# Hybrid encoder layer on one core: output projection by seven block products, second norm in two token halves, first weight sums spread through the recurrent heads

## What is computed

```python
mod = silu(c) @ w_ada + b_ada                      # shift, scale, gate, twice
h = rms_norm(x, norm_mix_pre) * (1 + sc1) + sh1
aq, ak, av, hq, hf_f, hf_b, hi, hg = split(h @ w_in)
o_att = attention_group(aq, ak, av, q_norm, k_norm)         # 8 heads, 1024 columns
o_hg = hgrn2_group(hq, hf_f, hf_b, hi, hg, ...)             # 8 recurrent heads, 1024 columns
mix = concatenate([o_att, o_hg]) @ w_out           # 512 tokens x 2048 by 2048 x 2048
x = x + g1 * rms_norm(mix, norm_mix_post)
h = rms_norm(x, norm_ffn_pre) * (1 + sc2) + sh2    # the second norm
x = x + g2 * rms_norm(conv_glu_ffn(h), norm_ffn_post)
```

## Time and profile before

| | |
|---|---|
| median of 3 runs | 2378.76 us (2375.49 to 2380.01) |
| span of the profiled execution | 2375.8 us |
| TensorE busy | 98% |
| VectorE busy | 79% |
| ScalarE busy | 47% |
| last head's loop and output projection | 840.4 to 1034.1 us |
| seam and first up rows | 1034.1 to 1075.2 us |

### The profile page before, as it was taken

One profiled execution on the slowest core, in us unless ns is written; L12 is line 12 of the kernel. 1 busy time (PEld: TensorE's weight loads), 2 busy tenths in 40 slices (PEclk: granted clock), 3 DMA queues, 4 the chain that ended last, 5 costly groups with the idle time before them and its releaser, 6 DMA issues.

```text
span 2375.8 us, 37218 instructions
## 1 busy us (share of the span) xinstructions
PE 2334.7 (98%) x13671; PEld 2025.8 (85%) x13671; DVE 1878.8 (79%) x2447; ACT 1104.8 (47%) x1517; POOL 128.6 (5%) x207
## 2 busy tenths in 40 slices
PE   6999999999999999999999999999999999999998
PEld 3577778888888877878999999999999998888887
DVE  5875667887777873267799999999999998888777
ACT  4266744334443353254444444444444445555554
POOL 1010000000000000000000000000000000001100
PEclk9999999999999999999999999999999999999999
DMA  9952456666666734336555555555555559779966
GB/s 366 346 157 85 133 180 208 215 219 212 207 211 198 234 89 169 98 124 159 146 140 146 145 144 143 144 142 139 141 145 145 142 176 329 251 207 285 279 226 224
DMA packets 378834, 442.47 MB, mean 186 GB/s; under 512 B 14876, under 2 KB 295716, under 8 KB 376448
## 3 DMA queue, kind: packets, MB, share of 16 engines
...
...
## 4 chain that ended last, share of the span: by engine, by line
PE 87%; DVE 5%; DMA 3%; ACT 2%; issue 2%; SPq 0%; DVEq 0%; ACTq 0%
PE bank L2132 26%; PE bank L2134 26%; PE bank L2133 26%; DMA ADA<-in_w_ada_dram 2%; PE bank L2295 2%; DVE ACC L1373 2%; DMA AB_raw<-in_w_ada_dram 1%; PE bank L2198 1%; DVE ZZ L1577 1%; PE bank L2375 1%; PE bank L2314 1%; PE bank L2189 1%; DVE W_lo L1332 0%; PE bank L2063 0%; DVE AB_acc L1636 0%
## 5 line engine op out<-in xcount | busy, mean ns | idle before, releaser
L2132 PE MATMUL bank<-H_lo,W_hi 128*128 128x256 f32 (+1 forms) x1832 | 635.7, 347 | 0.0
L2134 PE MATMUL bank<-H_hi,W_lo 128*128 128x256 f32 (+1 forms) x1832 | 613.6, 335 | 0.0
L2133 PE MATMUL bank<-H_hi,W_hi 128*128 128x256 f32 (+1 forms) x1832 | 613.2, 335 | 0.0
L2132 PEld LDWEIGHTS bank<-H_lo,W_hi 128*128 128x128 f32 x1832 | 349.3, 191 | 35.8 <-issue 6.2
L2133 PEld LDWEIGHTS bank<-H_hi,W_hi 128*128 128x128 f32 x1832 | 349.3, 191 | 35.7 <-issue 6.2
L2134 PEld LDWEIGHTS bank<-H_hi,W_lo 128*128 128x128 f32 x1832 | 348.8, 190 | 35.6
L2132 PE MATMUL bank<-T_lo,W_hi 128*128 128x256 f32 x1280 | 362.2, 283 | 0.0
L2133 PE MATMUL bank<-MGR,W_hi 128*128 128x256 f32 x1280 | 362.2, 283 | 0.0
L2134 PE MATMUL bank<-MGR,W_lo 128*128 128x256 f32 x1280 | 362.2, 283 | 0.0
L2132 PEld LDWEIGHTS bank<-T_lo,W_hi 128*128 128x128 f32 x1280 | 245.8, 192 | 0.0
L2133 PEld LDWEIGHTS bank<-MGR,W_hi 128*128 128x128 f32 x1280 | 245.8, 192 | 0.0
...
## 6 DMA issues: line engine op xcount, KB each, us to landing
AB_raw<-in_w_ada_dram SPq DMA_DIRECT2D x128, 512.0 KB, 4.4
UB<-in_w_up_dram SPq DMA_DIRECT2D x100, 512.0 KB, 4.1
W_raw<-in_w_in_dram SPq DMA_DIRECT2D x90, 512.0 KB, 4.8
t_dram<-in_w_down_dram POOLq DMA_DIRECT2D x88, 512.0 KB, 8.1
DRAW<-in_w_down_dram SPq DMA_DIRECT2D x66, 512.0 KB, 5.8
W_raw<-in_w_up_dram SPq DMA_DIRECT2D x56, 512.0 KB, 3.9
ADA<-in_w_ada_dram SPq DMA_DIRECT2D x48, 512.0 KB, 9.0
W_raw<-in_w_down_dram SPq DMA_DIRECT2D x44, 512.0 KB, 6.1
```

The costliest lines, as they stand in the source:

```text
L2132: pe.matmul(acc, st_hi, mv_lo, start=start, stop=False, skip_group_check=on)
L2133: pe.matmul(acc, st_hi, mv_hi, start=False, stop=False, skip_group_check=on)
L2134: return pe.matmul(acc, st_lo, mv_hi, start=False, stop=stop, skip_group_check=on)
```

## The change

The output projection is one 2 x 2 block product: the mix rows are split into attention and recurrent rows and into left (0 to 255) and right tokens, the weights into four blocks of 1024 x 1024. Seven products of such blocks replace eight. Each of the 56 units (`OUT`, product and row tile) is 12 matmuls of 512 columns. Products 1, 6, 5, 3 gather in the banks `CHAIN_A`, 7, 4, 2 in `CHAIN_C`. Four of the left operands are differences or sums of mix rows, made in place by VectorE (`combine`); in `PIECES` both these and their high and low parts (`CH`, `CL`) are cut into pieces. Three right operands are sums of weight blocks, made in DRAM (`o5_dram`, `o6_dram`, `o7_dram`) by 56 transfers on POOL: 48 in the recurrent heads, one every 4/3 units (24 plain, 24 adding), and the last eight, which turn `o6_dram` into the operand of product 4, after the last head. The 22 plain copies for `t2_dram` go from the heads into the up-projection's loop, three transfers per two column tiles there instead of two. In the last head TensorE has 60 output steps instead of 56, VectorE and ScalarE split 15 units instead of 8. Raw buffers are five, three of them in the head's first part.

Products 1 and 6 and 5 are kept in SBUF by ScalarE (`keep_chain`) and added by VectorE at the end of product 7. The right tokens' output is complete with product 4, so their norm, residual, sum of squares, scaling and transposes stand among the last output units. The left tokens' follow as before, but the up rows now come twice, first for the right tokens, then for the left, with 256 columns each. The filler matmuls at the seam are gone, and so is the gate's transpose between the first and second block: it stands in the head's loop at g = 71.

```diff
-U_UP = U_OUT + 32
+OUT = ([(1, k) for k in range(8)] + [(6, k) for k in range(7)] + [(7, 0), (6, 7), (7, 1)] + [(5, k) for k in range(8)]
+       + [(7, k) for k in range(2, 8)] + [(3, 0), (3, 1)] + [(4, k) for k in range(8)] + [(3, k) for k in range(2, 8)]
+       + [(2, k) for k in range(8)])
+OUT_END = {p: max(v for v, (q, k) in enumerate(OUT) if q == p) + 1 for p in range(1, 8)}
+OUT_SLOT = {1: 0, 6: 1, 7: 2, 5: 3, 3: 0, 2: 1, 4: 3}
+PIECES = ((1, 0, 2), (1, 2, 4), (1, 4, 8), (7, 0, 4), (7, 4, 8), (6, 0, 4), (6, 4, 7), (5, 0, 4), (6, 7, 8), (5, 4, 8),
...
+OUT_REGION = 15
+OUT_LAST = 2
+TILE_ORDER = (2, 3, 0, 1)
...
-    XR = at("XR", [P, TT, D], F32, WK)
+    XR = [at(f"XR{tt}", [P, D], F32, WK + o * KB) for tt, o in enumerate((16, 56, 48, 24))]
+    CH = [at(f"CH{n}", [P, 8, 256], F32R, 8 * n * KB) for n in range(4)]
+    CL = [at(f"CL{n}", [P, 8, 256], F32R, (32 + 8 * n) * KB) for n in range(4)]
+    Y_P1 = at("Y_P1", [P, 2, 1024], F32, WK + 16 * KB)
+    Y_U = at("Y_U", [P, 2, 1024], F32, WK + 48 * KB)
+    Y_V = at("Y_V", [P, 2, 1024], F32, WK + 56 * KB)
...
+        OUT_STEPS = [g for g in range(56) if g not in (35, 41, 47, 53)] + [57, 60, 65, 70, 73, 75, 77, 79]
+        assert len(OUT_STEPS) == 4 * OUT_REGION
...
+            def out_sum(n):
+
+                phase, k = n // 8, n % 8
+                top, low = slice(k * P, (k + 1) * P), slice((8 + k) * P, (9 + k) * P)
+                if phase == 0:
+                    pool.dma_start(o6_dram[k], w_out[0, top, 0:1024]).then_inc(o6_landed, 16)
+                elif phase == 1:
+                    pool.dma_start(o7_dram[k], w_out[0, top, 1024:2048]).then_inc(o7_landed, 16)
+                elif phase == 2:
+                    pool.wait_ge(o6_landed, o6_count + 8 * 16)
+                    pool.dma_start(o6_dram[k], w_out[0, top, 1024:2048], accum_op=ALU.add).then_inc(o6_landed, 16)
+                elif phase == 3:
+                    pool.wait_ge(o7_landed, o7_count + 8 * 16)
+                    pool.dma_start(o7_dram[k], w_out[0, low, 1024:2048], accum_op=ALU.add).then_inc(o7_landed, 16)
+                elif phase == 4:
+                    pool.wait_ge(o6_landed, o6_count + 2 * 8 * 16)
+                    pool.dma_start(o5_dram[k], o6_dram[k]).then_inc(o5_landed, 16)
+                elif phase == 5:
+                    pool.wait_ge(o5_landed, o5_count + 8 * 16)
+                    pool.dma_start(o6_dram[k], w_out[0, low, 1024:2048], accum_op=ALU.add).then_inc(o6_landed, 16)
+                else:
+                    pool.wait_ge(o6_landed, o6_count + 3 * 8 * 16)
+                    pool.wait_ge(lo_ready, U_OUT + OUT_END[6])
+                    pool.dma_start(o6_dram[k], w_out[0, low, 0:1024], accum_op=ALU.add).then_inc(o6_landed, 16)
+
+            for n in range(48):
+                pool.wait_ge(unit_used, U_HG + 10 + n * 4 // 3)
+                out_sum(n)
             pool.wait_ge(gate_rows, 1)
             pool.dma_start(gate_dram[0].rearrange("(r n) -> r n", n=P), JO[0:KT, 0:P]).then_inc(gate_stored, 16)
...
+            load_x(3)
+            pool.wait_ge(chain_added, 8)
+            load_x(2)
+            load_x(1)
+            pool.wait_ge(chain_kept, 16)
+            pool.wait_ge(xr_landed, 16)
...
+            def combine(n):
+
+                product, k0, k1 = PIECES[n]
+                a11, a21 = MX[:, k0:k1, left], MX[:, k0:k1, right]
+                a12, a22 = MX[:, 8 + k0:8 + k1, left], MX[:, 8 + k0:8 + k1, right]
+                if product == 7:
+                    ins = dve.tensor_tensor(a11, a11, a21, ALU.subtract)
+                elif product == 5:
+                    dve.wait_ge(o_done, k1)
+                    ins = dve.tensor_tensor(a21, a22, a21, ALU.subtract)
+                else:
+                    dve.wait_ge(o_done, k1)
+                    dve.wait_ge(mix_lo, {6: 5, 3: 9}[product])
+                    ins = dve.scalar_tensor_tensor(a11, a11, -1.0, a22 if product == 6 else a12, ALU.mult, ALU.subtract)
+                ins.then_inc(mix_sum, 1)
+
...
+            MIX_LO_AT = {7: 2, 14: 3, 18: 4, 23: 5, 28: 6, 40: 7}
+            COMBINE_AT = {9: 3, 15: 4, 19: 5, 24: 6, 34: 7}
...
+                if g in OUT_STEPS and OUT_STEPS.index(g) % 4 == 2:
+                    split_lo_out(OUT_STEPS.index(g) // 4 + LEAD)
...
+                if v == OUT_END[7]:
+                    dve.wait_ge(unit_used, U_OUT + OUT_END[7])
+                    dve.wait_ge(chain_kept, 12)
+                    for b in range(4):
+                        bank = PB[CHAIN_C[b]][:, :]
+                        blk = slice(b % 2 * 512, (b % 2 + 1) * 512)
+                        dve.tensor_tensor(mg_block(b, 1), bank, Y_V[:, b // 2, blk], ALU.add).then_inc(chain_added, 1)
+                        dve.tensor_tensor(bank, bank, Y_U[:, b // 2, blk], ALU.add).then_inc(chain_added, 1)
+                if v == 37:
...
+                if v == 42:
+                    dve.wait_ge(unit_used, U_OUT + OUT_END[4])
+                    for b in range(4):
+                        gate_bank(CHAIN_C[b], 2 + b // 2, b % 2)
+                    sum_mix(0, 6)
+                    sum_mix(1, 8)
+                    make_x1(0, 4)
+                if v == 43:
+                    make_x1(1, 6)
+                if v == 45:
...
+            sum_mix(2, 14)
+            h2_low(14)
+            make_x1(2, 12)
+            dve.wait_ge(unit_used, U_OUT + len(OUT))
+            for b in (2, 3):
+                dve.wait_ge(mg_squared, 12 + b + 1)
+                gate_bank(CHAIN_C[b], 1, b - 2)
+            sum_mix(3, 16)
             split_lo(0, 4, U_UP + 2)
-            for kt in range(KT):
-                if kt == 3:
-                    split_lo(0, 4, U_UP + 3)
-                dve.wait_ge(h2_ready, kt + 1)
-                if kt % 2:
-                    dve.tensor_copy(by_tile(H_hi[:, kt, :]), h2_row(kt)).then_inc(h2_hi_dve, 1)
-                    dve.wait_ge(h2_hi_dve, kt // 2 + 1)
-                else:
-                    dve.wait_ge(h2_hi_act, kt // 2 + 1)
...
-            def out_step(v, s):
-
-                cb, k = v // 8, v % 8
...
+                bank = PB[(CHAIN_C if product in (7, 4, 2) else CHAIN_A)[b]]
+                t, w = slice(b // 2 * P, (b // 2 + 1) * P), slice(b % 2 * 512, (b % 2 + 1) * 512)
+                opens = product in (1, 7)
+                return three_passes(bank[:, :], CH[n][:, k, t], CL[n][:, k, t], W_hi[:, slot, w], W_lo[:, slot, w],
+                                    opens and k == 0, opens and k == 7, not opens)
...
+            for v in range(OUT_REGION, len(OUT) - OUT_LAST):
+                for b in range(4):
+                    ins = out_step(v, b)
+                    if b == 3:
                         ins.then_inc(unit_used, 1)
-                    if half == 1 and kt == KT - 1:
-                        mid.then_inc(unit_used, 1)
+                    n = 4 * (v - 49) + b
+                    if n >= 0 and n % 3 == 2:
+                        turn_h2(n // 3 * 2)
+                        turn_h2(n // 3 * 2 + 1)
+
+            for r in range(2):
+                for v in range(len(OUT) - OUT_LAST, len(OUT)):
+                    for b in (2 * r, 2 * r + 1):
+                        ins = out_step(v, b)
+                    if r:
                         ins.then_inc(unit_used, 1)
-
-            for kt in range(KT):
-                if kt in (0, KT // 2):
-                    pe.wait_ge(x1_scaled, TT + (1 if kt else 0))
-                if kt == 0:
-                    pe.wait_ge(mg_ready, 4 * TT)
-                    pe.wait_ge(mg_squared, 4 * TT)
-                if kt >= 4:
-                    pe.wait_ge(h2_ready, kt - 3)
-                for tt in range(TT):
-                    ins = pe.transpose(PB[4 + kt % 4][:, tt * P:(tt + 1) * P], MG[:, tt, kt * P:(kt + 1) * P], ident[:, :])
-                ins.then_inc(h2_turned, 1)
-                if kt >= ROW_LAG:
-                    up_row(kt - ROW_LAG)
-            for kt in range(KT - ROW_LAG, KT):
-                up_row(kt)
+                    elif v == len(OUT) - 1:
+                        ins.then_inc(mix_tile_done, 1)
```

565 lines of the change are left out of this document (374 added, 191 removed).

## The result

| | before | after |
|---|---|---|
| median | 2378.55 us (2375.49 to 2380.01) | 2423.76 us (2417.31 to 2431.93) |
| ratio, 95% interval | | 1.0191 (1.0168 to 1.0214) |
| span of the profiled execution | 2375.8 us | 2429.3 us |

The changed kernel is slower by 1.9%. The forecast was 2370.2 us and its range ended at 2382. The profiled execution of the changed kernel took 2431.9 us, 8 above its median, so lengths read from this profile are somewhat larger than the median's difference of 45.2 us.

What follows compares the result with a forecast made beforehand. TensorE, busy 98%, was taken as the bound, with VectorE next. Gains of -27.9 us, then +4.3, +5.5, +4.5 and +5, sum to -8.6 us: span 2367.2, time 2370.2 us, range 2356 to 2382 us.

Steps and rivals of the forecast that it cites:

- The transfers in the heads: Recurrent heads: 48 new transfers replacing 22 copies delay loads TensorE waits for, +5 us, bounds -2 and +25.
- sign of being wrong: Recurrent heads: the prediction would be wrong if TensorE waits there more than 10 us in all.
- The ada loads become the bound: Rival, recurrent heads: two-buffer ada loads landing above 5.6 us set the pace, +21.6 in place of +5, 2386.8 us; chance 0.13.
- Block products: Output projection: 96 of 768 matmuls go, -21.8 us; a wait for the gate's transposes goes, -0.7 us.
- VectorE in the last head: Last recurrent head: more weight splitting and combinations on VectorE delay TensorE, +4.3 us, bounds 2 to 7.
- Waits in the other products: Output projection: TensorE waits for weight units after products 4, 3 and 7, +5.5 us, bounds 1 and 11.
- clock term: After three new TensorE waits (product 4, row 8, left half's first row): lower clock, 3 x 1.5 = +4.5 us, bounds 0 and 6.
- The third row of sums: Rival, output projection: late adding transfers make product 4 start 7 us late, 2377.2 us, no difference; chance 0.12.
- The seam: Last output matmul to end of up rows: 41.1 us becomes 32.8 plus 2.9 of moved transposes, -5.4 us.
- The 22 copies moved into the up-projection, at nothing: Feed-forward loop: 66 transfers in 44 steps, where TensorE never waited for a transfer; no cost in the sum.

Runs made afterwards that it cites:

- run with bursts: Changed kernel with all 48 transfers in eight bursts of six, each when a head's eighth weight unit is used, instead of evenly paced: 2388.48 us, ratio 1.0045.
- one change of order: Changed kernel, transfers in attention stage and seven bursts, weight units split first, third and fourth up weight units split before the last residual step: 2366.91 us, ratio 0.9958.
- Without transfers: Changed kernel without the 48 transfers in the recurrent heads, units reading plain blocks, last eight transfers plain copies: 2373.71 us, ratio 0.9979.

## Why the prediction was wrong

**The transfers in the heads** is the step that failed: +5 us in the sum (bounds -2 and +25), 59.3 measured against none, 54.2 against before (50 and 45 by the medians). The prediction's own sign of being wrong, TensorE waiting more than 10 us in the heads, came: 37.3. Three things in the step were wrong.
- The price of 0.08 us per us of DMA time was taken from 18 copies at the start of a head and carried over to 48 at any time in it. I had one sample of when, and took it for a rate. The run with bursts shows that the same transfers cost 16 us in one place and 58 in another, counted to the end of the eighth head.
- The average share (0.87 expected) was taken as room. It was 0.74, lower than I thought, and the heads were lengthened all the same.
- The earlier trace rows had the mechanism: two ada loads of 6.97 and 5.36 us in a row, with VectorE's scaling behind them. I read it as a rate for one burst; with a transfer every 9.6 us most pairs of loads, one every 7.2 us, meet one.

**The ada loads become the bound** was the right mechanism, with a chance of 0.13, and its price was low by more than half: 21.6 us. It let only adding transfers count, for 3.2 heads, at a landing of 6.5 and 6.8 us a head. Plain ones cost too (29 us for 48), single loads took 8 us and more while the median stayed at 4.7, and the slow clock came on top, some 15 us. The threshold of 5.6 us was held against the median; the loads that TensorE waited for, 7.93, 5.65 and 8.36, are above it one by one. The one thing held against the rival, the share under 1, is what failed above.

The rule of the Trainium skill, "DMA: Bandwidth & Descriptors", "Queues, rings and completion order", that queues are served in turn, packet by packet, I took to mean that a load gets half of the engines and lands 1.4 us later at most. The trace doesn't agree with that reading: beside adding transfers loads took 7.93 and 8.36 us, 3.5 to 4 more than 4.4, and beside the burst at 548.3 us they had 25.9% of the engines' time. Turns by packets are not halves of the time, because packets aren't equally long. In the earlier trace rows, which I had read as agreement, the loads have 5974 packets and the adding transfers 3022 at the same share: 0.16 and 0.31 us each, as an estimate from packets and shares. Beside that burst it is 0.03 us for a packet of the weight loads and again 0.31 for an adding one.

**Block products, -21.8 and -0.7**: 96 matmuls fewer at 0.227 us stood in the order and weren't in doubt. From 958.96 on, 41 units and the moved turns (2.9) would take 41 x 12 x 0.227 + 2.9 = 114.6 us and took 130.1.

**VectorE in the last head, +4.3** (bounds 2 to 7): before, the first matmul behind the loop starts at

```profile
896.44 0.39 PE L2132 MATMUL bank<-W_lo,H_hi 128*128 128x512 f32 x1
```

so the loop went from 56.0 us to 62.1, 6.1 more, of which 2.7 are the four steps: +3.4, near the forecast.

**Waits in the other products, +5.5** (bounds 1 to 11): of the 130.1 - 114.6 = 15.5 us too many, 10.0 are waits. Another 1.6 are the slow clock behind the longest, for which the forecast had 1.5 in its clock term, and 3.9 lie in the matmuls around the waits and in other small steps. The wait after product 4 (unit 44) is there, 3.73 us for 3.8; after product 7 it was 0.66 for 1.0, after product 3 none for 0.7. The 5.5 us of waits that I hadn't looked for stand at 963.37 (a low part), 969.71 (product 6 being kept), 977.10, 1000.87 and 1004.68 (`W_lo`; the last two after product 5). The third row of sums wasn't late: the first unit of product 4 waited those 0.66 us.

**The seam, -5.4, and its clock, +3.0**: 41.1 became 36.1, where 32.8 + 3.0 = 35.8 was the forecast. The two waits at the ninth row were 2.35 and 2.91, the predicted place and kind. This walk with durations was the best step. What it didn't ask is whether they need be there: one change of order took 3.9 us off.

**The 22 copies moved into the up-projection, at nothing**: the rest took 3.6 us more. In the old kernel with these transfers it was 1.4, and 1.6 to 6.8 in the others. Its spread is as large as itself, and I have no run that isolates it, so a price isn't shown.

The sum without the transfers' term was -13.6 us. Without transfers the ratio is 0.9979, 5 us: some 9 are missing. For the last head and the projection the forecast came to -8.3 (the clock after product 4 counted); -1.4 was measured in the changed kernel and -3.0 without transfers, where the last eight transfers are plain copies and the waits at 1000.87 and 1004.68 are gone. So 5 to 7 of the 9 are there. What the rest is stays open.
